# The first stage's preparation reordered over banks and engines, and attention values on two banks

## The chip, the cores and the metric

The kernel runs on one core of one Trainium2 chip. The metric is the device time of one execution in microseconds; the median of the runs is compared. One execution was taken by the hardware profiler; its times are counted from the first instruction of its span.

## The reference

The program computes two transformer-like blocks on x, 512 tokens by 1024, all in float32. The change touches the beginning of the first block:

```python
h = concatenate([lead, meta, x])                 # 16 meta tokens are real
a = rmsnorm(h, g_mix)
proj = einsum('bld,de->ble', a, w_in)            # 1024 x 3584, seven parts of 512 columns
sb_q, sb_k, sb_v, hg_q, hg_f, hg_i, hg_g = split(proj)
# stick-breaking attention, 8 heads of 64:
w = where(valid, exp(log_beta + log_tail), 0)
o = einsum('bhts,bhsd->bhtd', w, v)
```

Behind it come a gated linear recurrence on the other four parts, an output product, a mixture of 32 experts, and a second block (convolution, state-space scan, feed-forward). None of these is changed.

## The kernel before

Engines are programmed by hand: every engine has its own instruction list, in a fixed order, and they meet at semaphores. The eight PSUM banks of 512 float32 per partition are `banks[0]` to `banks[7]`.

**First stage (`stage_a`).** A float32 product is made of three float32r products: each operand is split in a high part (a rounded copy, ScalarE) and a low part (the difference, VectorE). The 512 tokens are four tiles of 128 rows, the meta tokens a fifth (`TILES`, L131). For each tile ScalarE squares and sums the row (L216) and takes the root (L219); VectorE takes the reciprocal (L307) and multiplies row, root and norm weights `gbc` into one of two `xn` buffers (L311); TensorE turns the tile by eight 128x128 transposes (L366) into banks 6 and 7; ScalarE copies each bank as `aT_hi` (L244), and VectorE subtracts to get `aT_lo` (L299). As all tiles use banks 6 and 7, a tile's turn waits until the lower part of the one before is made (L363).

The weights `w_in` come in 14 units of 1 MB (`units`), loaded by SP into three `raw` buffers (L164), split by ScalarE in `make_hi` (L238) and by VectorE in `make_lo` (L293) into two pairs `whi`, `wlo`. SP loads unit u once `make_lo` of unit u-3 is done (L156). On TensorE all five turns come first, then unit zero (L382 on), then the small vectors' four transposes (`vectors`, L354), then the other units. Unit zero and one are the 512 columns of q.

The order on ScalarE before: DMA of the meta rows (L191), DMA of the norm weights (L192), five times square and root, four constants for the attention (L224 to L228), fourteen DMAs that bring small vectors into `vrow` (L232), then the copies of the turned tiles, with the high part of unit zero behind tile 1 and of unit one behind tile 2. Then, unit by unit, the evacuation of the products; behind unit zero's stand two sigmoids of a gate constant (L280), behind each unit's the high part of the unit two further on. VectorE waits for the norm weights first, and its order is norm of tile j, lower part of tile j-1, low part of unit j-3. GpSimd makes masks at the start and then is free.

**Attention (first part of the next stage).** Eight heads, each in three pieces of 384, 384 and 512 columns, so 24 pieces. A piece's scores go into one of `RING` = 6 banks (L481 to L493), ScalarE takes three functions of it (`front`, L554), VectorE makes sums and splits them (`sums`, L658), TensorE adds the tails into the same bank (`tails`, L495), and ScalarE takes the exponential into `ww` (`weights`, L574), upon which the bank is free. TensorE runs three pieces ahead with the scores. The products with v of a head (`values`, L513) all go into bank 7, `O`, and wait until VectorE has copied the earlier head out (`out_evacuate`, L687). Bank 6 holds the meta tokens' scores.

Of the kernel before, what the change touches and what calls it, by code (L numbers as in the profile page):

```python
# [5 lines left out]
ALU = mybir.AluOpType  # L6
ACT = mybir.ActivationFunctionType
AX = mybir.AxisListType
F32 = mybir.dt.float32
# [4 lines left out]
P = 128  # L14
T = 512
NEVER = 2.0 ** 30
NT = T // P
D = 1024
KD = D // P
META = 16  # L20
# [50 lines left out]
def stage_a(nc, dram, g, sem, banks):  # L71
# [5 lines left out]
    with ExitStack() as keep:  # L77
        def sb(name, shape, dt=F32, ctx=None):
# [19 lines left out]
            "it xor xf up ge mask never".split())}  # L98
        s_x = [sem(f"a_x{i}") for i in range(NT)]
        s_raw = [sem(f"a_raw{i}") for i in range(3)]  # L100
        with ExitStack() as tmp:
# [45 lines left out]

            block = tmp.enter_context(nc.Block())

            @block.sync  # L150
            def _(sp):
                for i in range(NT):
                    sp.dma_start(h[:, i, :], x_t[:, i, :]).then_inc(s_x[i], 16)
                for u, (n, what, turned, half) in enumerate(units):
                    if u >= 3:
                        sp.wait_ge(s["wlo"], u - 2)  # L156
                    c = n * 512
                    if turned:
                        src = w_in[:, :, c + half * 256:c + half * 256 + 256]
                        dst = raw[u % 3].rearrange("p (k c) -> p k c", k=KD)  # L160
                    else:
                        src = w_in[:, half * 4:half * 4 + 4, c:c + 512]
# [24 lines left out]

            @block.scalar
            def _(act):
                act.wait_ge(s["hm0"], 1)  # L190
                act.dma_start(hm[0:META, :], dram["meta_tokens"]).then_inc(s["meta"], 16)  # L191
                act.dma_start(gbc, dram["g_mix"][0].partition_broadcast(P)).then_inc(s["gbc"], 16)  # L192
                srcs = {
                    "lb": dram["lb_logits"].rearrange("l (c p) -> (l c) p", p=P),
                    "sb_gain": dram["sb_gain"].rearrange("l (c p) -> (l c) p", p=P),
                    "hg_gain": dram["hg_gain"].rearrange("l (c p) -> (l c) p", p=P),
                    "gate_b": dram["gate_b_2"].rearrange("l (c p) -> (l c) p", p=P),
                    "glu_b": dram["glu_b_2"].rearrange("l (c p) -> (l c) p", p=P),
                    "dw_b": dram["conv_dw_b_2"].rearrange("l (c p) -> (l c) p", p=P),
                    "ln_g": dram["conv_ln_g_2"].rearrange("l (c p) -> (l c) p", p=P),  # L200
                    "ln_b": dram["conv_ln_b_2"].rearrange("l (c p) -> (l c) p", p=P),
                    "pw_b": dram["conv_pw_b_2"].rearrange("l (c p) -> (l c) p", p=P),
                    "ssm_b": dram["ssm_conv_b_2"].rearrange("l (c p) -> (l c) p", p=P),
                    "norm_g": dram["ssm_norm_g_2"].rearrange("l (c p) -> (l c) p", p=P),
                    "dw_w_a": dram["conv_dw_w_2"][0].rearrange("k (c p) -> (k c) p", p=P)[0:128],
                    "dw_w_b": dram["conv_dw_w_2"][0].rearrange("k (c p) -> (k c) p", p=P)[128:CONV_K * 8],
                    "ssm_w": dram["ssm_conv_w_2"][0].rearrange("k (c p) -> (k c) p", p=P),
                }

                act.wait_ge(s["eps"], 1)  # L210
                for j, i in enumerate(TILES):
                    if i == NT:
                        act.wait_ge(s["meta"], 16)
                    else:
                        act.wait_ge(s_x[i], 16)
                    nc.scalar.activation(sq[:, :], hm if i == NT else h[:, i, :], ACT.Square,  # L216
                                         accum_out=ssq[:, i:i + 1]).then_inc(s["ssq"], 1)
                    act.wait_ge(s["ssq"], j + 1)
                    nc.scalar.activation(rt[:, i:i + 1], ssq[:, i:i + 1], ACT.Sqrt, bias=eps[:, 0:1],  # L219
                                         scale=1.0 / D).then_inc(s["rt"], 1)  # L220
                act.wait_ge(s["never"], 2)
# [7 lines left out]
                for t, tile in enumerate(VEC_TILES):  # L229
                    at = 0  # L230
                    for name, n in tile:
                        act.dma_start(vrow[at:at + n, t, :], srcs[name]).then_inc(s["vec"], 16)  # L232
                        at += n
                def make_hi(u):
                    act.wait_ge(s_raw[u % 3], 16 * (u // 3 + 1))
                    if u >= 2:
                        act.wait_ge(s["wused"], u - 1)
                    nc.scalar.copy(whi[u % 2][:, :], raw[u % 3]).then_inc(s["whi"], 1)  # L238


                for j, i in enumerate(TILES):
                    for half in range(2):
                        act.wait_ge(s["tr"], 2 * j + half + 1)
                        nc.scalar.copy(aT_hi[:, 4 * half:4 * half + 4, i * P:i * P + P],  # L244
                                       banks[6 + half][:, :].rearrange("p (k t) -> p k t", k=4)).then_inc(s["hi"], 1)
                    if 1 <= j < 3:
                        make_hi(j - 1)
# [38 lines left out]
            def _(dve):  # L286
# [9 lines left out]
                def lower(j, i):  # L296
                    for half in range(2):
                        dve.wait_ge(s["hi"], 2 * j + half + 1)
                        nc.vector.tensor_tensor(aT_lo[:, 4 * half:4 * half + 4, i * P:i * P + P],  # L299
                                                banks[6 + half][:, :].rearrange("p (k t) -> p k t", k=4),  # L300
# [3 lines left out]
                dve.wait_ge(s["gbc"], 16)  # L304
                for j, i in enumerate(TILES):
# [7 lines left out]
                    if j >= 1:  # L313
                        lower(j - 1, TILES[j - 1])
                    if j >= 3:
                        make_lo(j - 3)
                lower(4, TILES[4])
# [29 lines left out]
            def _(pe):  # L347
# [12 lines left out]
                for j, i in enumerate(TILES):  # L360
                    pe.wait_ge(s["xn"], j + 1)
                    for half in range(2):
                        if j >= 1:  # L363
# [5 lines left out]
                pe.wait_ge(s["lo"], 10)  # L369
# [68 lines left out]
        NP, WIDTH, AHEAD, RING = 3 * SB_HEADS, 1280, 3, 6  # L438
        s = {n: sem("b_" + n) for n in (
            "zm z ab u l k q t w o oev con conr qs qhi own vb kb vr vm abm um lm spm tm wm om mo osq ossq ort ors on f kx q1 dec tab").split()}  # L440
        with ExitStack() as tmp:
# [17 lines left out]
            ZM, O = pall[:, 6, :], pall[:, 7, :]  # L459
# [17 lines left out]
            def _(pe):  # L477
# [53 lines left out]
                for n in range(NP):  # L531
# [3 lines left out]
                    if n == 0:  # L535
# [5 lines left out]
                        mm(O, pick[:, :, :].rearrange("k h s -> k (h s)"), v_nat[0:META, NT, :], start=True,  # L541
# [108 lines left out]
            def _(dve):  # L650
# [30 lines left out]
                def values_meta():  # L681
                    dve.wait_ge(s["vr"], 1)
                    dve.wait_ge(s["own"], 3)
                    V.tensor_tensor(vb[:, :, :], O.rearrange("p (h d) -> p h d", h=SB_HEADS),
                                    own_rows[:, :].unsqueeze(2).to_broadcast([P, SB_HEADS, SB_DIM]), ALU.mult).then_inc(s["vm"], 1)

                def out_evacuate(hd):  # L687
                    dve.wait_ge(s["o"], hd + 1)
                    V.tensor_copy(o_sb[:, :, hd * SB_DIM:hd * SB_DIM + SB_DIM],
                                  O[:, 0:NT * SB_DIM].rearrange("p (i d) -> p i d", i=NT)).then_inc(s["oev"], 1)  # L690
# [2328 lines left out]
```

## Time and profile before

| | |
|---|---|
| Median of three runs | 2304.44 us (2299.78 to 2311.39) |
| The profiled execution | 2295.25 us, its span 2293.2 us |
| TensorE busy | 2061.0 us, 90% of the span |
| VectorE, ScalarE, GpSimd busy | 1363.3, 1069.2, 167.6 us |
| Mean granted TensorE clock | 0.941 |
| First product of unit zero | 35.35 us |
| Attention starts | 224.2 us |

The profile page gives busy times over the whole span; the rows below are from stretches of it. PE is TensorE's matmul queue, PEld its weight loads, DVE VectorE, ACT ScalarE, POOL GpSimd, SP SyncE, and a trailing q is the engine's instruction queue (DMA issues). PEclk is the share of full TensorE clock that was granted.

### The profile page before, as it was taken

How to read it: one execution, taken by the hardware profiler on the slowest of the kernel's cores; microseconds unless marked ns; L12 is line 12 of the kernel's file. 1: busy time of each engine (PE TensorE's matmuls, PEld its weight loads, DVE VectorE, ACT ScalarE, POOL GpSimd, SP SyncE). 2: the span in 40 equal slices, each digit the busy share in tenths (PEclk: the TensorE clock that was granted, in tenths of full speed). 3: DMA queues.
4: the chain of work that ended last, by engine and by line, in shares of the span. 5: the costliest groups of instructions: out<-in, count | busy, mean ns of one | idle time of the engine just before them, and what ended most of it. 6: DMA issues, size and time to landing. Idle time of an engine off the chain costs nothing. (4 is left out here: it accounts for less than half of the span.)

```text
span 2293.2 us, 25099 instructions
## 1 busy us (share of the span) xinstructions
PE 2061.0 (90%) x10173; PEld 1640.2 (72%) x10173; DVE 1363.3 (59%) x1511; ACT 1069.2 (47%) x1253; POOL 167.6 (7%) x129
## 2 busy tenths in 40 slices
PE   5999987879999999947799999988698988999997
PEld 4887666756666666636688888877487866888786
DVE  4111777489989988943398888876533254333213
ACT  4223533468888888833334455545241233222212
POOL 0000100012213222200000000000000000000000
PEclk9999799989999999976999999999899988999999
DMA  4220003379999999951333333322222212333221
GB/s 149 86 74 0 1 1 121 131 271 407 405 402 400 402 403 402 363 200 51 93 86 96 94 93 92 93 74 56 68 79 92 92 56 83 96 105 93 90 94 56
DMA packets 201776, 346.84 MB, mean 151 GB/s; under 512 B 13587, under 2 KB 149259, under 8 KB 184251
## 3 DMA queue, kind: packets, MB, share of 16 engines
q1 hardware_dynamic: 193508, 333.16, 41.4%
q0 software_dynamic: 5120, 8.40, 1.1%
q10 hardware_dynamic: 3031, 3.65, 0.5%
q8 instruction: 82, 1.34, 0.2%
q14 instruction: 35, 0.29, 0.0%
HBM read 340.91 MB, written 12.65 MB: 154 GB/s over the span
## 5 line engine op out<-in xcount | busy, mean ns | idle before, releaser
L1453 DVE TENSOR_TENSOR wlo_e<-raw_e,whi_e 128x2048 fp32r<-128x2048 f32 x190 | 431.8, 2288 | 56.2 <-ACT whi_e L1378 55.6
L1750 DVE TENSOR_TENSOR w_lo<-w_raw,w_hi 128x2048 fp32r<-128x2048 f32 x89 | 203.8, 2290 | 321.1 <-ACT w_hi L1742 321.1
L1378 ACT CAST whi_e<-raw_e 128x2048 fp32r<-128x2048 f32 x188 | 359.3, 1912 | 73.5 <-PE pall L1529 44.9
L1742 ACT CAST w_hi<-w_raw 128x2048 fp32r<-128x2048 f32 x89 | 169.4, 1904 | 428.4 <-PE pall L50 414.2
L48 PE MATMUL pall<-hT_hi,w_lo 128*128 128x512 f32 x864 | 347.8, 403 | 22.9 <-DVE xbc L2294 10.3
L49 PE MATMUL pall<-hT_lo,w_hi 128*128 128x512 f32 x864 | 341.6, 395 | 0.0
L50 PE MATMUL pall<-hT_hi,w_hi 128*128 128x512 f32 x864 | 341.1, 395 | 0.0
L1528 PE MATMUL pall<-whi_e,xs 128*128 128x512 f32 x512 | 210.2, 411 | 3.0 <-DVE xs L1458 3.0
L48 PEld LDWEIGHTS pall<-hT_hi,w_lo 128*128 128x128 f32 x864 | 165.9, 192 | 59.7 <-DVE xbc L2294 10.6
L1529 PE MATMUL pall<-wlo_e,xs 128*64 128x512 f32 x512 | 206.1, 403 | 0.0
L50 PEld LDWEIGHTS pall<-hT_hi,w_hi 128*128 128x128 f32 x864 | 165.5, 192 | 35.5
L49 PEld LDWEIGHTS pall<-hT_lo,w_hi 128*128 128x128 f32 x864 | 166.0, 192 | 34.6 <-issue 0.5
L1528 PEld LDWEIGHTS pall<-whi_e,xs 128*128 128x128 f32 x512 | 99.5, 194 | 54.8 <-issue 4.5
L2279 DVE SCALAR_TENSOR_TENSOR mixed<-yT,cols,mixed 128x512 f32<-128x512 f32 x180 | 126.4, 748 | 0.0
L48 PE MATMUL pall<-w_hi,hT_lo 128*128 128x256 f32 (+1 forms) x320 | 100.0, 313 | 8.8 <-DVE hT_lo L2740 8.4
L48 PE MATMUL pall<-whi_e,hT_lo 128*64 128x512 f32 x256 | 101.4, 396 | 5.7 <-issue 4.1
L50 PE MATMUL pall<-whi_e,hT_hi 128*64 128x512 f32 x256 | 101.1, 395 | 0.0
L49 PE MATMUL pall<-wlo_e,hT_hi 128*64 128x512 f32 x256 | 100.8, 394 | 0.0
L49 PE MATMUL pall<-w_lo,hT_hi 128*128 128x256 f32 (+1 forms) x320 | 98.8, 309 | 0.0
L50 PE MATMUL pall<-w_hi,hT_hi 128*128 128x256 f32 (+1 forms) x320 | 98.6, 308 | 0.0
L2897 DVE TENSOR_TENSOR mixed<-mixed,pall 128x512 f32<-128x512 f32 x22 | 15.1, 688 | 139.9 <-PE pall L50 139.9
L1529 PEld LDWEIGHTS pall<-wlo_e,xs 128*64 128x64 f32 x512 | 70.9, 138 | 21.6
(468 smaller groups left out, 3807.3 us busy)
## 6 DMA issues: line engine op xcount, KB each, us to landing
raw_e<-in_w_expert_up_dram SPq DMA_DIRECT2D x64, 1024.0 KB, 11.1
raw_e<-in_w_expert_down_dram SPq DMA_DIRECT2D x64, 1024.0 KB, 11.5
raw_e<-in_w_expert_gate_dram SPq DMA_DIRECT2D x64, 1024.0 KB, 11.5
w_raw<-in_w_in_dram SPq DMA_DIRECT2D x80, 512.0 KB, 5.9
w_raw<-in_w_gate_up_dram SPq DMA_DIRECT2D x44, 512.0 KB, 5.1
w_raw<-in_w_down_dram SPq DMA_DIRECT2D x22, 512.0 KB, 4.1
mixed<-in_w_in_dram SPq DMA_DIRECT2D x10, 1024.0 KB, 5.1
A<-acs_rows SPq DMA_DIRECT2D x8, 1024.0 KB, 5.0
```

Source lines behind the costliest of these rows:

```text
L48: nc.tensor.matmul(out, w_lo, m_hi, start=start, stop=False)
L49: nc.tensor.matmul(out, w_hi, m_lo, start=False, stop=False)
L50: return nc.tensor.matmul(out, w_hi, m_hi, start=False, stop=stop)
L1378: nc.scalar.copy(whi[j], raw[j]).then_inc(sem_hi, 1)
L1453: nc.vector.tensor_tensor(wlo[j], raw[j], whi[j].bitcast(F32), ALU.subtract).then_inc(sem_lo, 1)
L1528: mm(out, x[:, kk, :], k4(whi[j])[:, k, :], start=kk == 0, stop=False, skip_group_check=True)
L1529: last = mm(out[0:SLOTS, :], x[:, kk, 0:SLOTS], k4(wlo[j])[:, k, :], start=False, stop=kk == KD - 1, skip_group_check=True)
L1742: self.nc.scalar.copy(self.hi[i][:, :], self.raw[i][:, :]).then_inc(self.s_hi, 1)
L1750: (engine or self.nc.vector).tensor_tensor(self.lo[i][:, :], self.raw[i][:, :], self.hi[i][:, :].bitcast(F32), ALU.subtract).then_inc(self ...
L2279: ins = V.scalar_tensor_tensor(mixT[:, c, :], src, col("dw_w_a", k * KD + c), mixT[:, c, :], ALU.mult, ALU.add)
L2897: V.tensor_tensor(hd, sg, banks[(2 * c + 1) % 8], ALU.mult).then_inc(s["hd"], 1)
```

## The change

In the first stage the norm weights' DMA becomes ScalarE's first instruction, followed by a load of the function table that has square and root. The small vectors' fourteen DMAs move from ScalarE's queue to SP's, behind the loads of the first three units. The four tiles of tokens are turned into own pairs of banks (0 and 1, 2 and 3, 4 and 5, 6 and 7), so the turns no longer wait for the lower parts; the meta tile is turned behind unit zero. ScalarE makes the high part of unit zero behind tile 0's copies, the constants come last. The low part of unit zero is made by GpSimd. In the attention the ring has five banks, and the values alternate between bank 5 and bank 7.

```diff
+            def turn_bank(j):
+                return 2 * j if j < NT else 6
+            def made_lo(u):
+                return (s["wlo0"], 1) if u == 0 else (s["wlo"], u)
             @block.sync
...
+                    if u == 3:
+                        for t, tile in enumerate(VEC_TILES):
+                            at = 0
+                            for name, rows_n in tile:
+                                sp.dma_start(vrow[at:at + rows_n, t, :], srcs[name]).then_inc(s["vec"], 16)
+                                at += rows_n
                     if u >= 3:
-                        sp.wait_ge(s["wlo"], u - 2)
+                        sp.wait_ge(*made_lo(u - 3))
...
+                pool.wait_ge(s["whi"], 1)
+                nc.gpsimd.tensor_tensor(wlo[0][:, :], raw[0], whi[0][:, :].bitcast(F32), ALU.subtract).then_inc(s["wlo0"], 1)
             @block.scalar
             def _(act):
+                act.dma_start(gbc, dram["g_mix"][0].partition_broadcast(P)).then_inc(s["gbc"], 16)
+                nc.scalar.preload_act_table_set("sqrt_and_others")
                 act.wait_ge(s["hm0"], 1)
                 act.dma_start(hm[0:META, :], dram["meta_tokens"]).then_inc(s["meta"], 16)
-                act.dma_start(gbc, dram["g_mix"][0].partition_broadcast(P)).then_inc(s["gbc"], 16)
...
+                root(0)
+                root(1)
+                root(2)
+                root(3)
+                upper(0)
+                make_hi(0)
+                upper(1)
+                upper(2)
+                upper(3)
+                root(4)
+                make_hi(1)
+                upper(4)
                 act.wait_ge(s["never"], 2)
...
             @block.vector
...
+                dve.wait_ge(s["gbc"], 16)
+                normed(0)
+                normed(1)
+                normed(2)
+                lower(0)
+                normed(3)
+                lower(1)
+                lower(2)
+                lower(3)
+                normed(4)
+                make_lo(1)
+                lower(4)
             @block.tensor
...
+                def turn(j):
                     pe.wait_ge(s["xn"], j + 1)
                     for half in range(2):
-                        if j >= 1:
-                            pe.wait_ge(s["lo"], 2 * (j - 1) + half + 1)
                         for k in range(4):
-                            last = nc.tensor.transpose(banks[6 + half][:, k * P:k * P + P],
+                            last = nc.tensor.transpose(banks[turn_bank(j) + half][:, k * P:k * P + P],
...
+                for j in range(NT):
+                    turn(j)
+                pe.wait_ge(s["lo"], 2 * NT)
                 o = 0
                 for u, (n, what, turned, half) in enumerate(units):
                     if u == 1:
+                        turn(NT)
                         vectors()
                     if u == 2:
                         pe.wait_ge(s["cols"], 1)
-                    pe.wait_ge(s["wlo"], u + 1)
+                        pe.wait_ge(s["lo"], 2 * NT + 2)
+                    pe.wait_ge(*made_lo(u))
...
-        NP, WIDTH, AHEAD, RING = 3 * SB_HEADS, 1280, 3, 6
+        NP, WIDTH, AHEAD, RING = 3 * SB_HEADS, 1280, 3, 5
...
-            ZM, O = pall[:, 6, :], pall[:, 7, :]
+            ZM, O_OF, OM = pall[:, 6, :], (pall[:, 5, :], pall[:, 7, :]), pall[:, 7, :]
...
                 def values(hd):
                     pe.wait_ge(s["w"], 3 * hd + 3)
-                    if hd == 0:
+                    if hd == 1:
                         pe.wait_ge(s["vm"], 1)
-                    else:
-                        pe.wait_ge(s["oev"], hd)
-                    w = ww[hd % 2]
+                    if hd >= 2:
+                        pe.wait_ge(s["oev"], hd - 1)
+                    w, O = ww[hd % 2], O_OF[hd % 2]
```

`root(j)` is square and root of tile j, `upper(j)` and `lower(j)` its high and low copies, `normed(j)` its reciprocal and product into `xn`, with the same instructions and waits as before; `turn_bank` gives their bank. `srcs`, the table of the vectors' places in memory, is unchanged and now stands ahead of the engines' lists. The meta part's helpers name bank 7 as `OM`, and `out_evacuate` reads `O_OF[hd % 2]`.

## Rows read from the trace of the kernel before

**Rows 1.** Busy time in a stretch: from:to, us, then busy (count) by engine, PEclk, DMA.

```profile
100.00:150.00 50.00, 50.00 (x235) 41.80 (x235) 9.17 (x4) 15.65 (x16) 0.00 (x0) 1.00 0.28 91
```

**Rows 2.** Timeline, start to first squares: start us, us, engine line operation out<-in.

```profile
0.79 1.82 SPq L153 DMA_DIRECT2D h<-in_x_dram  x4
...
2.47 0.46 ACTq L192 DMA_DIRECT2D hg_nat<-in_g_mix_dram  x1
2.65 2.63 SPq L164 DMA_DIRECT2D mixed<-in_w_in_dram  x2
...
4.36 1.28 ACT L216 ACT_TABLE_LOAD   x1 [4.36 <-DMA h<-in_x_dram]
...
8.31 1.04 ACT L216 ACTIVATE sq_a<-h 128x1024 f32<-128x1024 f32 x1
...
11.04 1.04 ACT L216 ACTIVATE sq_a<-h 128x1024 f32<-128x1024 f32 x1
```

**Rows 3.** Timeline, from the norm weights to unit zero's first product.

```profile
10.43 0.16 DVE L307 RECIPROCAL rs_a<-rt_a 128x1 f32<-128x1 f32 x1 [8.45 <-DMA hg_nat<-in_g_mix_dram]
...
10.63 1.28 DVE L311 SCALAR_TENSOR_TENSOR xn_a<-h,rs_a,hg_nat 128x1024 f32<-128x1024 f32 x1
...
12.06 1.94 PE L366 MATMUL pall<-ident,xn_a 128*128 128x128 f32 x8 [12.06 <-DVE xn_a L311]
...
13.76 0.54 ACTq L232 DMA_DIRECT2D vrow<-in_lb_logits_dram  x1
...
19.48 1.07 ACT L244 CAST aT_hi<-pall 128x512 fp32r<-128x512 f32 x2 [4.50 <-issue]
...
23.40 1.90 ACT L238 CAST whi_a<-mixed 128x2048 fp32r<-128x2048 f32 x1
...
25.82 1.29 DVE L299 TENSOR_TENSOR aT_lo<-pall,aT_hi 128x512 fp32r<-128x512 f32 x2 [0.20 <-ACT aT_hi L244]
...
35.35 0.80 PE L393 MATMUL pall<-aT_hi,wlo_a 128*128 128x512 f32 x1 [1.96 <-DVE aT_lo L299]
```

**Rows 4.** ScalarE's DMA queue, 7 to 10 us; landings of norm weights, x, units zero and one.

```profile
q10 hardware_dynamic: 142, 0.52, 46.5%
...
DMA to landing us min/median/max: 7.9/7.9/7.9
...
DMA to landing us min/median/max: 3.5/5.2/8.0
...
DMA to landing us min/median/max: 10.7/11.9/13.2
```

**Rows 5.** Timeline, GpSimd's products in the attention and VectorE beside them.

```profile
255.06 4.55 POOL L641 TENSOR_TENSOR q<-hqT,hfT 128x2048 f32<-128x2048 f32 x1 [27.36 <-ACT hfT L582]
255.12 4.77 DVE L673 CAST qh<-qq 128x512 fp32r<-128x512 f32 x1
...
262.35 0.56 DVE L664 SCALAR_TENSOR_TENSOR qq<-pall,ll 128x384 f32<-128x384 f32 x1
```

**Rows 6.** Timeline, between unit zero and unit one, and unit two's low part.

```profile
47.73 0.60 PE L354 MATMUL pall<-ident,vrow 128*128 128x128 f32 x4
...
48.08 0.48 PE L393 MATMUL pall<-aT_hi,wlo_a 128*128 128x512 f32 x1
...
52.43 2.28 DVE L293 TENSOR_TENSOR wlo_a<-raw_a,whi_a 128x2048 fp32r<-128x2048 f32 x1
```

**Rows 7.** Busy time in two stretches of the attention, three pieces (one head) each.

```profile
265.80:281.60 15.80, 15.32 (x47) 10.86 (x46) 10.63 (x23) 6.18 (x12) 0.00 (x0) 0.53 0.01 1
281.60:290.17 8.57, 8.57 (x46) 6.21 (x46) 5.17 (x12) 6.16 (x12) 0.00 (x0) 1.00 0.00 0
```

**Rows 8.** Timeline of the attention: a wait of the values; weights, then scores.

```profile
267.61 4.50 PE L523 MATMUL pall<-v_nat,ww 128*128 128x64 f32 x20 [0.48 <-DVE mixed L689]
...
295.81 0.47 ACT L579 ACTIVATE ww<-pall 128x384 f32<-128x384 f32 x1
...
297.65 0.33 PE L486 MATMUL pall<-keep_r,ident_r 128*128 128x384 f32 x1
```

More of the change, by code:

```diff
@@ L97, in stage_a @@
             "x meta vec gbc ident ones eps hm0 ssq rt rs xn tr hi lo vtr cols lbd lb whi wlo wused out evac "
-            "it xor xf up ge mask never".split())}
+            "it xor xf up ge mask never wlo0".split())}
         s_x = [sem(f"a_x{i}") for i in range(NT)]
@@ L146, in is_meta_turned @@
                 return what in ("k", "hf")
+            def turn_bank(j):
+                return 2 * j if j < NT else 6
             block = tmp.enter_context(nc.Block())
+            def made_lo(u):
+                return (s["wlo0"], 1) if u == 0 else (s["wlo"], u)
+            srcs = {
+                "lb": dram["lb_logits"].rearrange("l (c p) -> (l c) p", p=P),
+                "sb_gain": dram["sb_gain"].rearrange("l (c p) -> (l c) p", p=P),
+                "hg_gain": dram["hg_gain"].rearrange("l (c p) -> (l c) p", p=P),
+                "gate_b": dram["gate_b_2"].rearrange("l (c p) -> (l c) p", p=P),
+                "glu_b": dram["glu_b_2"].rearrange("l (c p) -> (l c) p", p=P),
+                "dw_b": dram["conv_dw_b_2"].rearrange("l (c p) -> (l c) p", p=P),
+                "ln_g": dram["conv_ln_g_2"].rearrange("l (c p) -> (l c) p", p=P),
+                "ln_b": dram["conv_ln_b_2"].rearrange("l (c p) -> (l c) p", p=P),
+                "pw_b": dram["conv_pw_b_2"].rearrange("l (c p) -> (l c) p", p=P),
+                "ssm_b": dram["ssm_conv_b_2"].rearrange("l (c p) -> (l c) p", p=P),
+                "norm_g": dram["ssm_norm_g_2"].rearrange("l (c p) -> (l c) p", p=P),
+                "dw_w_a": dram["conv_dw_w_2"][0].rearrange("k (c p) -> (k c) p", p=P)[0:128],
+                "dw_w_b": dram["conv_dw_w_2"][0].rearrange("k (c p) -> (k c) p", p=P)[128:CONV_K * 8],
+                "ssm_w": dram["ssm_conv_w_2"][0].rearrange("k (c p) -> (k c) p", p=P),
+            }
             @block.sync
@@ L186, in _, with root @@
                                         pattern=[[1, P]], channel_multiplier=-1).then_inc(s["never"], 1)
+                pool.wait_ge(s["whi"], 1)
+                nc.gpsimd.tensor_tensor(wlo[0][:, :], raw[0], whi[0][:, :].bitcast(F32), ALU.subtract).then_inc(s["wlo0"], 1)
             @block.scalar
             def _(act):
+                act.dma_start(gbc, dram["g_mix"][0].partition_broadcast(P)).then_inc(s["gbc"], 16)
+                nc.scalar.preload_act_table_set("sqrt_and_others")
                 act.wait_ge(s["hm0"], 1)
                 act.dma_start(hm[0:META, :], dram["meta_tokens"]).then_inc(s["meta"], 16)
-                act.dma_start(gbc, dram["g_mix"][0].partition_broadcast(P)).then_inc(s["gbc"], 16)
[L193 to L208, printed above, removed]
                 act.wait_ge(s["eps"], 1)
-                for j, i in enumerate(TILES):
+                def root(j):
+                    i = TILES[j]
                     if i == NT:
@@ L215, in _ @@
                         act.wait_ge(s_x[i], 16)
+                    if j >= 1:
+                        act.wait_ge(s["ssq"], j)
                     nc.scalar.activation(sq[:, :], hm if i == NT else h[:, i, :], ACT.Square,
@@ L220, in _, with make_hi, upper @@
                                          scale=1.0 / D).then_inc(s["rt"], 1)
+                def make_hi(u):
+                    act.wait_ge(s_raw[u % 3], 16 * (u // 3 + 1))
+                    if u >= 2:
+                        act.wait_ge(s["wused"], u - 1)
+                    nc.scalar.copy(whi[u % 2][:, :], raw[u % 3]).then_inc(s["whi"], 1)
+                def upper(j):
+                    i = TILES[j]
+                    for half in range(2):
+                        act.wait_ge(s["tr"], 2 * j + half + 1)
+                        nc.scalar.copy(aT_hi[:, 4 * half:4 * half + 4, i * P:i * P + P],
+                                       banks[turn_bank(j) + half][:, :].rearrange("p (k t) -> p k t", k=4)).then_inc(s["hi"], 1)
+                root(0)
[10 more added lines that the diff above has]
+                upper(4)
                 act.wait_ge(s["never"], 2)
@@ L228, in _ @@
                                      scale=0.0)
[L229 to L247, printed above, removed]
                 def evacuate(o):
@@ L294, in make_lo, with lower @@
                                             ALU.subtract).then_inc(s["wlo"], 1)
-                def lower(j, i):
+                def lower(j):
+                    i = TILES[j]
                     for half in range(2):
@@ L299, in lower, with normed @@
                         nc.vector.tensor_tensor(aT_lo[:, 4 * half:4 * half + 4, i * P:i * P + P],
-                                                banks[6 + half][:, :].rearrange("p (k t) -> p k t", k=4),
+                                                banks[turn_bank(j) + half][:, :].rearrange("p (k t) -> p k t", k=4),
                                                 aT_hi[:, 4 * half:4 * half + 4, i * P:i * P + P].bitcast(F32),
                                                 ALU.subtract).then_inc(s["lo"], 1)
-                dve.wait_ge(s["gbc"], 16)
-                for j, i in enumerate(TILES):
+                def normed(j):
+                    i = TILES[j]
                     dve.wait_ge(s["rt"], j + 1)
@@ L312, in _ @@
                                                    gbc, ALU.mult, ALU.mult).then_inc(s["xn"], 1)
-                    if j >= 1:
[L314 to L317, printed above, removed]
+                dve.wait_ge(s["gbc"], 16)
[10 more added lines that the diff above has]
+                lower(4)
                 dve.wait_ge(s["vtr"], 1)
@@ L358, in _ @@
                 pe.wait_ge(s["ident"], 2)
-                for j, i in enumerate(TILES):
+                def turn(j):
                     pe.wait_ge(s["xn"], j + 1)
                     for half in range(2):
-                        if j >= 1:
-                            pe.wait_ge(s["lo"], 2 * (j - 1) + half + 1)
                         for k in range(4):
-                            last = nc.tensor.transpose(banks[6 + half][:, k * P:k * P + P],
+                            last = nc.tensor.transpose(banks[turn_bank(j) + half][:, k * P:k * P + P],
                                                        xn[j % 2][:, (4 * half + k) * P:(4 * half + k + 1) * P], ident[:, :])
                         last.then_inc(s["tr"], 1)
-                pe.wait_ge(s["lo"], 10)
+                for j in range(NT):
+                    turn(j)
+                pe.wait_ge(s["lo"], 2 * NT)
                 o = 0
@@ L540, in _ @@
                         pe.wait_ge(s["vb"], 1)
-                        mm(O, pick[:, :, :].rearrange("k h s -> k (h s)"), v_nat[0:META, NT, :], start=True,
+                        mm(OM, pick[:, :, :].rearrange("k h s -> k (h s)"), v_nat[0:META, NT, :], start=True,
                            stop=True).then_inc(s["vr"], 1)
@@ L683, in values_meta @@
                     dve.wait_ge(s["own"], 3)
-                    V.tensor_tensor(vb[:, :, :], O.rearrange("p (h d) -> p h d", h=SB_HEADS),
+                    V.tensor_tensor(vb[:, :, :], OM.rearrange("p (h d) -> p h d", h=SB_HEADS),
                                     own_rows[:, :].unsqueeze(2).to_broadcast([P, SB_HEADS, SB_DIM]), ALU.mult).then_inc(s["vm"], 1)
@@ L689, in out_evacuate @@
                     V.tensor_copy(o_sb[:, :, hd * SB_DIM:hd * SB_DIM + SB_DIM],
-                                  O[:, 0:NT * SB_DIM].rearrange("p (i d) -> p i d", i=NT)).then_inc(s["oev"], 1)
+                                  O_OF[hd % 2][:, 0:NT * SB_DIM].rearrange("p (i d) -> p i d", i=NT)).then_inc(s["oev"], 1)
                 def keys(e):
```

## The prediction

> **What bounds the kernel now.** I read the table of stretches first. In the first stage's products (100 to 150 us) TensorE is busy for all 50.00 us, so a product is never waited for; its first product starts only at 35.35 us [rows 1, 3]. Every microsecond by which that start moves forward is therefore a microsecond of the time, as long as nothing later eats it. Next the timeline of the stretch before it. The order there is: x lands in four tiles, ScalarE squares them, VectorE waits for the norm weights until 10.43, TensorE turns the first tile at 12.06, and then ScalarE, which has to copy the turned tile, is issuing DMAs: the first of the vectors' DMAs goes out at 13.76 and the first copy comes at 19.48 [rows 2, 3]. After that the five tiles go through one pair of banks, one after another, with the splitting of units zero and one in between. Last the attention: a head takes 8.57 us at granted clock 1.00, with TensorE busy throughout, and 15.80 us at 0.53 [rows 7]; TensorE bounds it too.
>
> **The first stage, step by step (times from the span's start).**
> 1. Norm weights. Their DMA goes out at 2.47 and lands 7.9 later, at 10.4; between 7 and 10 us its queue moved 0.52 MB and took 46.5% of the DMA engines [rows 2, 4], so once its turn comes it gets about half. After the change it is ScalarE's first instruction, near 1.0, and only the first tile of x is ahead. Shared with one or two tiles it lands at 5.5 to 6.5; with the latency of before, at 8.9. I take 6.2. The DMA was the wait of VectorE; what is late next is x.
> 2. Table. One load of 1.28 us stands behind the first tile's landing at 4.36 [rows 2]; a second one follows the first square. The change makes it one, done while x is in flight. The squares after the second load need none, so one set serves both functions. Worth nothing by itself: the fourth tile of x is issued near 2.2 and lands 8.0 later, at 10.2 [rows 2, 4], and with the weights ahead of it the sum of bytes up to there is the same. Squares come every 1.37 us ((11.04 - 8.31) / 2, [rows 2]), so the four roots are done at 10.2 + 1.4 = 11.6.
> 3. Splitting unit zero. ScalarE makes the upper halves of tile 0 (1.07 for two copies [rows 3]), to 12.7, and then the high part of unit zero. That waits for the load, which was issued at 2.65 and landed 10.7 later, at 13.35 [rows 2, 4]; x, weights and meta rows are ahead of it as before, so this stands. 13.35 + 1.90 for the copy [rows 3] = 15.3. GpSimd takes over the low part: it waits for this copy and has nothing queued behind; the nearest row is its product of the same 128x2048 shape, 4.55 us [rows 5]. 15.4 + 4.55 = 20.0, and TensorE starts unit zero at 20.1. Bounds: 19.4 if the load is in before ScalarE is free, 21.3 if GpSimd first waits for a VectorE instruction of 1.28 us.
> 4. The tiles beside it. VectorE norms tile 0 to 2 by 12.1, lowers tile 0 (1.29 for the pair, [rows 3]) to 13.4, and norms tile 3 (reciprocal 0.16, product 1.28) from 13.4 to 14.9. TensorE turns tile 3 in 1.94 [rows 3] to 17.0. ScalarE is free of unit zero at 15.3 and copies tiles 1 to 3 in 3 x 1.07, to 18.5; the last lowering ends at 19.2. So TensorE waits for GpSimd, by 0.8 us; that is the margin of these tiles.
> 5. The meta tile's turn moves behind unit zero, onto TensorE's path. The vectors' four turns take it from 47.73 to 48.08 [rows 6], 0.35; eight at that pace cost 0.7. Upper bound 1.94, the cold duration. Its norming (root five on ScalarE, 18.5 to 19.9) and unit one's halves (ScalarE to 21.8, VectorE to 24.1) lie under unit zero, which runs to 32.
> 6. What queues behind. ScalarE now waits for the meta tile's turn, and behind it stand the six 0.3 to 0.6 us copies it did early before, the evacuations of unit zero, the gate constants and then the high part of unit two. Before, unit two's low part started at 52.43 and took 2.28 [rows 6], done 6.6 after unit one's start at 48.08; unit zero, with its slow beginning, took 12.4 (35.35 to 47.73, [rows 3, 6]), unit one takes about 11. After the change about 2.3 us more stand in ScalarE's queue there, so it is done some 8.9 after: 2 us of slack are left. Cost nothing; if the cover fails, rival B.
> 7. The fourteen vector DMAs on SP's queue: issue time some 0.35 each, 10.2 to 15.2, then SP waits for GpSimd's part at 20.0. Unit three's load, behind them, took 5.0 us at that place before, so it lands at 25; its split is wanted after 44. The vectors are wanted at 32. Nothing.
> 8. The waits dropped between tiles (own banks) are contained in these times.
> Start of unit zero 35.35 - 20.1 = 15.25 earlier, less 0.7: 14.5. The half-speed products at the beginning of unit zero stay.
>
> **Attention.** Five banks in the ring instead of six: the scores of a piece wait for the weights of one piece later. The tightest place in a head: weights done at 295.81 + 0.47 = 296.28, the scores that will need them start at 297.65 [rows 8], 1.37 later; in the other two pieces of a head it is more. So this wait holds nobody: cost zero, and that is the upper end unless the order shifts. Two value banks: TensorE waited for the earlier head's evacuation once, 0.48 us, before the values at 267.61 [rows 8]; this wait goes. TensorE is the bound there, so 0.5 gained. The lower end is nothing.
>
> **Sum.** 14.5 + 0.5 = 15.0. The profiled execution took 2295.25 (span 2293.2); it becomes 2280.2. The median of the three runs shown is 2304.44, 9.2 above that execution, and 2289.4 is what I forecast for it.
>
> **A lock that speaks against it.** When GpSimd began its 4.55 us product at 255.06, VectorE's cast at 255.12 took 4.77, while the VectorE instruction with one operand in PSUM ran in 0.56 beside GpSimd's next products [rows 5]. By this the lowerings (one operand in PSUM) run beside GpSimd, but tile 3's norming has x and the weights, both in SBUF. The Trainium skill, "SBUF — State Buffer", section "SBUF: two separate sides", says the pair of ports that VectorE and GpSimd share is an exclusive lock, taken also by a VectorE instruction with two SBUF inputs, and whoever starts first holds it for the whole instruction; the trace's cast agrees, and for a norming no run here shows it.
>
> **Rivals.**
> A. GpSimd gets in first. If tile 3's norming starts after 15.4 instead of 13.6, it is held to 20.0: norm to 21.3, turn to 23.2, copy and lowering to 24.7. Start 4.6 later, gain 10.4: 2294.0. For it: the weights landing only at 8.9 (latency as before) puts that norming at 15.1 to 15.4, the very edge. Against: half of the queue's rate from 2 us on, and 1.8 us of room. 0.12.
> B. Unit two comes late: step 6 short of slack by 2 to 3 us. Gain 12.5: 2292. For it: ScalarE's queue is in order and the slack is my estimate. 0.08.
> C. Slower than before. The place is the attention: the stretch at half clock [rows 7] comes right behind the stall of [rows 5], and a shorter one stands at the stage's start. Each further head at it costs 15.80 - 8.57 = 7.2 us [rows 7]. It decides from the point where more than two heads (15.0 / 7.2) are added; if five that now run at full clock fall, +36 - 15 = +21: 2325. For it: the clock already falls twice in this stage. Against: full clock comes back at 281.6 under the same load, and the ring adds no idle time. 0.05 (slower), and 0.05 for one or two heads, which ends near no change.
> D. The other way: with the stages shifted, one head less at half clock, gain 22: 2282. 0.07.
> E. The forecast, 2289.4: 0.63.
>
> **Range and chances.** E alone, with a start between 19.4 and 21.3, the meta turn up to 1.94 and the runs' own spread of some 5 us: 2283 to 2296. Taking in A, B and D: 2279 to 2300. Of this kernel's runs (2299.78 to 2311.39) about 0.5%, 11.5 us, can be told from no change, so 2292.9 is the edge: E is above it only in one case of seven; A is just beyond, B just within. Faster 0.70, same 0.24, slower 0.06.
>
> **What would show it.** First product of unit zero at 20.1 (right from 19.4 to 21.3), released by GpSimd; weights landed by 6.5; one table load before the first square; tile 3's norming 1.28 us long, not 5; unit one's first product 14.5 earlier than 48.08; products of unit two without a gap; no wait of scores for weights; from there on the two traces run parallel, 15 us apart. Wrong if the start is later than 24, if TensorE stands still before unit two, or if the attention runs longer or shorter at a granted clock of 0.5 than before.

## The result and the profile after

The changed kernel takes 2277.41 us at the median of its first four runs (2271.61 to 2279.0) against 2302.11 for the kernel before; the ratio is 0.9893, 95% interval 0.9865 to 0.9921. Two repetitions gave 0.9929 [0.9907, 0.9951] and 0.9905 [0.9882, 0.9928]. Over all 16 runs of it the mean is 2278.8, over 60 runs of the kernel before 2298.5 (standard deviations 4.2 and 4.7): 19.6 us faster. The forecast was 2289.4, faster by 15.0, with 2279 as its lower end: the direction and the mechanism of the first stage came out, the time is 1.6 us under the range.

The profiled execution took 2279.0 us, its span 2276.8, 16.4 less than before. Its timeline, for [rows 2] and [rows 3]:

```profile
0.78 0.40 ACTq L221 DMA_DIRECT2D hg_nat<-in_g_mix_dram  x1
0.79 2.11 SPq L176 DMA_DIRECT2D h<-in_x_dram  x4
...
1.21 1.28 ACT L222 ACT_TABLE_LOAD   x1 [1.21 <-PEq L3047]
...
6.59 1.06 ACT L235 ACTIVATE sq_a<-h 128x1024 f32<-128x1024 f32 x1 [4.10 <-DMA h<-in_x_dram]
...
8.18 0.16 DVE L335 RECIPROCAL rs_a<-rt_a 128x1 f32<-128x1 f32 x1 [6.19 <-ACT rt_a L238]
...
9.81 5.31 PE L400 MATMUL pall<-ident,xn_a 128*128 128x128 f32 x24 [9.81 <-DVE xn_a L339]
...
12.56 1.06 ACT L251 CAST aT_hi<-pall 128x512 fp32r<-128x512 f32 x2
...
14.03 1.90 ACT L245 CAST whi_a<-mixed 128x2048 fp32r<-128x2048 f32 x1 [0.41 <-DMA mixed<-in_w_in_dram]
...
14.55 1.28 DVE L339 SCALAR_TENSOR_TENSOR xn_a<-h,rs_a,hg_nat 128x1024 f32<-128x1024 f32 x1
...
16.01 4.58 POOL L217 TENSOR_TENSOR wlo_a<-mixed,whi_a 128x2048 fp32r<-128x2048 f32 x1 [12.99 <-ACT whi_a L245]
...
16.44 3.68 DVE L327 TENSOR_TENSOR aT_lo<-pall,aT_hi 128x512 fp32r<-128x512 f32 x6 [0.60 <-ACT aT_hi L251]
...
20.74 0.76 PE L432 MATMUL pall<-aT_hi,wlo_a 128*128 128x512 f32 x1 [3.75 <-POOL wlo_a L217]
...
33.82 1.03 PE L400 MATMUL pall<-ident,xn_a 128*128 128x128 f32 x8
...
34.69 0.60 PE L390 MATMUL pall<-ident,vrow 128*128 128x128 f32 x4
...
35.04 0.48 PE L432 MATMUL pall<-aT_hi,wlo_a 128*128 128x512 f32 x1
```

The reader is to see that each link named in the prediction is there. VectorE's first wait ends with ScalarE's root, no longer with the weights' DMA. Tile 0's copies come at 12.56 instead of 19.48. ScalarE then waits for unit zero's load (14.03), GpSimd follows at 16.01, and unit zero starts at 20.74, released by GpSimd, with the lowerings done at 20.12. Behind it stand the meta tile's turn (33.82 to 34.69, 0.87) and the vectors. Two repetitions of the kernel start unit zero at 20.54 and 20.50.

Stretches of the same kernel: the first products of unit zero, the attention's first 13 us, and its second half-clock stretch, which answers to [rows 7].

```profile
20.70:25.10 4.40, 4.36 (x10) 3.46 (x11) 3.33 (x2) 1.31 (x1) 0.00 (x0) 0.50 0.73 238
...
211.21:224.00 12.79, 12.79 (x26) 6.46 (x27) 9.77 (x25) 8.66 (x17) 2.94 (x13) 0.60 0.01 1
...
245.50:267.60 22.10, 19.72 (x57) 13.35 (x57) 17.30 (x31) 9.81 (x19) 6.60 (x8) 0.61 0.00 1
```

How far ahead of the kernel before it is at each landmark: unit zero 14.6 us, unit one (48.08 - 35.04) 13.0, attention (224.23 - 211.21) 13.0, the recurrence behind it (325.09 - 311.66) 13.4, end of the span 16.4. The last 3.0 lie where nothing was changed: from the start of the recurrence to the end it takes 1968.1 us in `before` and 1965.1 here, but 1965.8 in `before_again` and 1968.5 in the two repetitions of the changed kernel. So they are scatter.

### The profile page after: what moved, and what is told of

Same layout as the page of the kernel before. It is cut to its first block and busy times, and to the rows that moved or that the text cites. A ratio compares the mean times of both kernels' runs of the same rounds, so it can differ in the third digit from the quotient of the medians.

```text
span 2276.8 us, 25098 instructions
## 1 busy us (share of the span) xinstructions
PE 2054.9 (90%) x10173; PEld 1636.9 (72%) x10173; DVE 1361.3 (60%) x1510; ACT 1066.6 (47%) x1252; POOL 173.3 (8%) x130
## 3 DMA queue, kind: packets, MB, share of 16 engines
HBM read 340.91 MB, written 12.65 MB: 155 GB/s over the span
## 5 line engine op out<-in xcount | busy, mean ns | idle before, releaser
L971 POOL DMA_INDIRECT xg<-m_rows,row_x x32 | 81.8, 2557 | 67.4 <-PE pall L1558 36.2
```

Of the source, the lines that this page charges most:

```text
L971: pool.indirect_dma_start(xg[0:SLOTS, :], None, m_rows, bass.IndirectOffsetOnAxis(g["row_x"][0:SLOTS, b:b + 1], 0), bounds_check=T - 1, oo ...
```

## The experiments

**Both kernels again, and each part alone.** The first two are the kernels unchanged; `first_only` is the first stage of the change with the attention of before, `att_only` the reverse (the diff shows the lines that set the banks; those that follow from them are left out):

```diff
 # first_only
+NP, WIDTH, AHEAD, RING = 3 * SB_HEADS, 1280, 3, 6
+ZM, O = pall[:, 6, :], pall[:, 7, :]
 # att_only: the kernel before, with
+NP, WIDTH, AHEAD, RING = 3 * SB_HEADS, 1280, 3, 5
+ZM, O_OF, OM = pall[:, 6, :], (pall[:, 5, :], pall[:, 7, :]), pall[:, 7, :]
```

> The kernel before, unchanged, as its own yardstick. Both theories: ratio to the kernel before 1.000. It also gives a second profile of it. Theory one (the true gain of the change is about 15, and the 24.7 between the medians comes from runs of the kernel before that differ by 20 us among themselves): the runs of this kernel scatter again over more than 10 us, and its second profile differs from the first in the lengths of half-clock stretches, not in the first 35 us, where unit zero starts again at 35.35 within 0.3. Theory two (the true gain is about 25): the profile of before, 2295.25, was a lucky run, and this one's profile is nearer to 2302.

> The changed kernel, unchanged, timed again. Theory one, gain of 15: ratio 0.9935, that is 2287 against 2302. Theory two, gain of 25: ratio 0.989. Unit zero starts at 20.7 within 0.3 in this profile too.

> The change's first stage with the attention of before (six score banks, one value bank). Theory one: 0.5 us slower than the full change, not to be told from it, ratio 0.994; unit zero at 20.7, attention start 13.0 earlier than 224.2, one 0.5 us wait of the values in front of an evacuation. Rival: the attention part is worth the missing 9 us, then this one is at 0.993 and the full change at 0.989.

> The kernel before with the attention part of the change alone (five score banks, two value banks). Theory one: ratio 1.000 (0.5 us faster), the values' wait for the evacuation gone, no wait of scores for weights. Rival: ratio 0.996, 9 us faster, visible as fewer or shorter half-clock stretches in the attention.

> The changed kernel a third time, to settle the size of its gain: 0.9893 [0.9865, 0.9921] at first, 0.9929 [0.9907, 0.9951] the second time. Gain of 16 (stage starts 13 to 14 us earlier, attention 1 to 3 by its clock): 0.993. Gain of 25: 0.989. In the profile unit zero starts at 20.6 within 0.3.

Measured: `before_again` 1.001 [0.9994, 1.0026] over 12 runs from 2293.69 to 2308.22; `after_again` 0.9929; `first_only` 0.9939 [0.9917, 0.9961]; `att_only` 0.9991 [0.9978, 1.0004]; `after_third` 0.9905. The kernel before scatters by 15 us in itself, so the first theory holds in that; but neither size is confirmed: the three ratios of the change mean 0.9909, about 21 us, between 15 and 25.

The first stage is most of the change: by the means, `first_only` is 14.1 us faster than the 24 runs of the kernel before beside it. The standard error, the expected error of such a difference from the scatter of its runs, is 2.1 us. The attention part is small and hard to see. The ratio of `att_only` includes no change, its mean is 3.1 us lower (standard error 1.3), and the changed kernel's mean is 4.6 lower than that of `first_only` (2.2). A gain of 9 us is ruled out.

Much of the scatter is the clock, and each run has its mean granted clock on record. The span times (1 - clock) is the time that a run loses to the half clock, about half the length of its stretches at 0.5. With this time taken off, `att_only` is 2.7 us faster than the 57 runs of the kernel before that have a clock (standard error 0.7). So the attention part is worth more than the 0.5 of the forecast. A part of it is the wait of the values for the earlier head's evacuation. It was 0.48 in `before` [rows 8], and here it is in `before_again` and in `first_only`, both with one value bank:

```profile
268.56 4.40 PE L523 MATMUL pall<-v_nat,ww 128*128 128x64 f32 x20 [1.99 <-DVE mixed L689]
...
255.08 4.50 PE L562 MATMUL pall<-v_nat,ww 128*128 128x64 f32 x20 [2.00 <-DVE mixed L728]
```

With two banks, in `att_only` and the changed kernel, the wait is gone (in `vec_moved`, with one bank, there is none either). In single profiles the attention's length (100.86 us in `before`, 101.20 in `before_again`, 100.45 in `att_only`; 100.45, 96.70 and 101.44 in the changed kernel) is too scattered to show the gain.

**The vectors' DMAs.** These two kernels and the next four were run once each; their times (2274.68 to 2296.65 us) differ by little more than the two kernels scatter, so they are read by the start of unit zero in their traces, and say nothing of the whole time. `vec_back` starts from the changed kernel, `vec_moved` from the kernel before; the loops are shortened here:

```diff
 # vec_back: taken from SP, and on ScalarE
                 root(3)
+                for t, tile in enumerate(VEC_TILES): ... act.dma_start(vrow[...], srcs[name])
                 upper(0)
 # vec_moved: taken from ScalarE, and on SP
+                    if u == 3:
+                        for t, tile in enumerate(VEC_TILES): ... sp.dma_start(vrow[...], srcs[name])
```

> The changed kernel with the vectors' fourteen DMAs on ScalarE again, ahead of tile 0's copies. My theory (before, ScalarE's DMA issues held the copies): root four is done at 12.6, the issues take 5.7 us (13.76 to 19.44 before), tile 0's copies start at 18.3, unit zero's high part at 19.3, GpSimd ends at 25.8, unit zero's first product at 26, 5.3 later than 20.7. Rival (the issues are hidden, the own banks or the earlier weights made the gain): 21 to 22.

> The kernel before with only the vectors' DMAs moved to SP. My theory: tile 0's copies start when the four constants are done, 15.0 instead of 19.48, and all that follows is 4.5 earlier: unit zero at 30.9 instead of 35.4. Rival (hidden): 35.

The timelines of `vec_back`, then of `vec_moved`:

```profile
12.37 0.53 ACTq L255 DMA_DIRECT2D vrow<-in_lb_logits_dram  x1
...
18.02 1.07 ACT L245 CAST aT_hi<-pall 128x512 fp32r<-128x512 f32 x2 [5.36 <-issue]
...
25.94 0.77 PE L431 MATMUL pall<-aT_hi,wlo_a 128*128 128x512 f32 x1 [2.59 <-POOL wlo_a L211]
```

```profile
15.03 1.04 ACT L246 CAST aT_hi<-pall 128x512 fp32r<-128x512 f32 x2
...
30.87 0.79 PE L395 MATMUL pall<-aT_hi,wlo_a 128*128 128x512 f32 x1 [1.97 <-DVE aT_lo L301]
```

Unit zero at 25.94 (26 expected) and 30.87 (30.9): ScalarE's DMA issues are worth 4.5 us from the one side and 5.2 from the other. "Idle until issue" in front of a copy is what such a wait looks like.

**The lock.** All three start from the changed kernel; `norm3_beside` was made to test rival A's mechanism, the others for a part of the change each:

```diff
 # norm3_beside (VectorE)
                 lower(0)
-                normed(3)
                 lower(1)
+                normed(3)
 # weights_late (ScalarE)
                 act.dma_start(hm[0:META, :], dram["meta_tokens"]).then_inc(s["meta"], 16)
+                act.dma_start(gbc, dram["g_mix"][0].partition_broadcast(P)).then_inc(s["gbc"], 16)
 # one_pair
-                return 2 * j if j < NT else 6
+                return 6
+                        if j >= 1:
+                            pe.wait_ge(s["lo"], 2 * (j - 1) + half + 1)
```

> The changed kernel with one swap in VectorE's order: tile 3's norming after tile 1's lowering, so that it meets GpSimd's 4.6 us product (16.0 to 20.6). Lock theory (rival A of the prediction): lowerings with a PSUM operand run beside GpSimd in their 0.65; the norming, both operands in SBUF, is held from 17.9 to 20.6 and the record is about 4 us long instead of 1.28; unit zero at 24.7. No lock for this instruction: 1.28 long, unit zero at 21.8.

> The changed kernel with the norm weights' DMA behind the meta rows' again, as before (issue near 2.4 us). My theory: they land near 10.3 instead of before 8.2; tile 0 is normed at 10.5 instead of 8.4, tile 3's norming starts at 16.7, inside GpSimd's product, is held to 20.6, and unit zero starts at 24.7. If the weights' order doesn't matter: 20.7. If it matters but nothing is held: 21.

> The changed kernel with all tiles turned into banks 6 and 7 and the waits on the lower parts back. My theory: each turn waits for the lowering before it, the last lowering ends near 22.9, unit zero at 23.0, 2.3 later. If own banks are worth nothing: 20.7; if they are the main part of the gain: 30 or later.

Timelines of `norm3_beside`, of `weights_late`, and of `one_pair`:

```profile
15.79 4.61 POOL L217 TENSOR_TENSOR wlo_a<-mixed,whi_a 128x2048 fp32r<-128x2048 f32 x1 [12.78 <-ACT whi_a L245]
16.23 1.29 DVE L327 TENSOR_TENSOR aT_lo<-pall,aT_hi 128x512 fp32r<-128x512 f32 x2 [2.02 <-ACT aT_hi L251]
...
17.62 3.85 DVE L339 SCALAR_TENSOR_TENSOR xn_a<-h,rs_a,hg_nat 128x1024 f32<-128x1024 f32 x1
...
24.90 0.79 PE L432 MATMUL pall<-aT_hi,wlo_a 128*128 128x512 f32 x1 [1.40 <-DVE aT_lo L327]
```

```profile
10.36 0.16 DVE L335 RECIPROCAL rs_a<-rt_a 128x1 f32<-128x1 f32 x1 [8.38 <-DMA hg_nat<-in_g_mix_dram]
...
16.44 4.59 POOL L217 TENSOR_TENSOR wlo_a<-mixed,whi_a 128x2048 fp32r<-128x2048 f32 x1 [13.42 <-ACT whi_a L245]
...
16.63 5.48 DVE L339 SCALAR_TENSOR_TENSOR xn_a<-h,rs_a,hg_nat 128x1024 f32<-128x1024 f32 x1
...
25.76 0.80 PE L432 MATMUL pall<-aT_hi,wlo_a 128*128 128x512 f32 x1 [1.62 <-DVE aT_lo L327]
```

```profile
15.91 4.63 POOL L217 TENSOR_TENSOR wlo_a<-mixed,whi_a 128x2048 fp32r<-128x2048 f32 x1 [12.89 <-ACT whi_a L245]
15.97 5.65 DVE L339 SCALAR_TENSOR_TENSOR xn_a<-h,rs_a,hg_nat 128x1024 f32<-128x1024 f32 x1 [1.53 <-PE pall L402]
...
28.29 0.79 PE L434 MATMUL pall<-aT_hi,wlo_a 128*128 128x512 f32 x1 [1.40 <-DVE aT_lo L327]
```

The norming lasts 1.28 us alone and 3.85, 5.48 and 5.65 when GpSimd started first: each time it ends 1.1 us behind GpSimd. The lowerings, one operand in PSUM, keep their pace (1.29 for the pair in `norm3_beside`, as before). The Trainium skill ("SBUF — State Buffer", "SBUF: two separate sides") has this as a lock held for the whole instruction; the three traces agree for a VectorE product of two SBUF operands. So rival A's mechanism is real and 4.2 us dear (24.90 against 20.74), and both the early weights and the own banks are needed to stay clear of it. My 24.7 for `weights_late` was 1.1 early: I let the norming end with GpSimd, at 20.6, and it ended at 22.11. My 23.0 for `one_pair` was wrong by 5.3: I had tile 3's norming at 15.8, before GpSimd. It came 0.06 behind it.

**GpSimd or VectorE for unit zero's low part.**

```diff
                 normed(3)
+                dve.wait_ge(s["whi"], 1)
+                nc.vector.tensor_tensor(wlo[0][:, :], raw[0], whi[0][:, :].bitcast(F32), ALU.subtract)
                 lower(1)
```

> The changed kernel with unit zero's low part on VectorE (behind tile 3's norming) instead of GpSimd. My theory: 2.28 us there from 16.0 to 18.3, then six lowerings of 0.62 to 22.0, unit zero at 22.2, so 1.5 later than 20.7: GpSimd is worth 1.5 us only. Rival (GpSimd's 4.6 us product is the bound and VectorE would beat it): 20.3 or earlier.

```profile
15.84 2.29 DVE L347 TENSOR_TENSOR wlo_a<-mixed,whi_a 128x2048 fp32r<-128x2048 f32 x1
18.05 3.67 DVE L325 TENSOR_TENSOR aT_lo<-pall,aT_hi 128x512 fp32r<-128x512 f32 x6
```

Unit zero at 21.77, 1.0 later than with GpSimd, not 1.5: VectorE needs 2.29 instead of 4.58 but then has the six lowerings (3.67) behind it.

**A faster version.** `spread` cuts GpSimd's products in the attention ([rows 5]), of which the first is shown; `spread_warm` also keeps TensorE busy before unit zero:

```diff
+                for e in range(HG_HEADS):
+                    pool.wait_ge(s["q"], 9 + 2 * e)
+                    gp.tensor_tensor(q1[:, e, :], hqT[:, e, :], hfT[:, e, META:TM], ALU.mult)
...
 # spread_warm, behind turn(3)
+                pe.wait_ge(s["lo"], 2)
+                for n in range(28):
+                    nc.tensor.transpose(banks[0][:, 0:P], ident[:, :], ident[:, :])
```

> The changed kernel, and in the attention GpSimd's products (4.55 + 2.13 + 3.8 us in one go, in whose lock VectorE stood 4.77 and 2.32 us) cut into pieces of at most 1.2 us and spread over pieces 8 to 23 by waiting for VectorE's progress. Theory (the stall makes the half-clock stretch behind it): no idle TensorE of over 1 us there, granted clock 1.00 from the ninth piece on, a head every 8.6 us; 10 us faster than the changed kernel, ratio to before 0.989. Rival (the clock falls there without the stall, or the cut products stall VectorE as long in sum): within 2 us of the changed kernel, 0.993.

> The spread kernel, and TensorE turns the identity 28 times into a free bank between tile 3's turn and unit zero (work that nothing reads). In the changed kernel it stands idle there from 17.0 to 20.74 and runs the first ten products of unit zero at granted clock 0.50, until 25.1. Theory (the idle time costs the clock): unit zero's products take 0.227 us each from the first on, unit one's first product comes near 32.6 instead of 34.5 to 35.5, 2.2 us gained: ratio to before 0.9865. Rival (the clock falls after the turns whatever follows): unit one's start stays at 34.5 or later.

`spread`: 2269.99 us, ratio 0.9875 [0.9852, 0.9897]; `spread_warm`: 2267.48 us, 0.9861 [0.9834, 0.9889]. The attention of `spread` in three stretches, and its first cut product:

```profile
210.40:223.00 12.60, 12.60 (x39) 6.21 (x39) 10.71 (x27) 11.20 (x22) 2.95 (x13) 1.00 0.00 1
223.00:245.00 22.00, 22.00 (x114) 15.89 (x114) 17.55 (x34) 19.35 (x38) 2.54 (x2) 1.00 0.00 1
245.00:267.00 22.00, 22.00 (x116) 15.55 (x115) 18.23 (x37) 15.10 (x30) 4.88 (x4) 1.00 0.00 0
...
237.83 1.27 POOL L682 TENSOR_TENSOR q<-hqT,hfT 128x512 f32<-128x512 f32 x1 [23.96 <-DVE ql L720]
```

In these stretches TensorE is busy throughout at full clock; from the attention's start to the recurrence it takes 85.4 us instead of 100.45. The whole kernel doesn't gain these 15 us. By the means `spread` is 8.5 us faster than the changed kernel (standard error 3.0). One reason stands in its profile: a new stretch at half clock in the recurrence, where work that took 43.8 us now takes 47.9:

```profile
334.00:344.40 10.40, 10.40 (x48) 9.85 (x49) 5.62 (x15) 1.76 (x3) 0.00 (x0) 0.51 0.01 2
```

`spread_warm` has this stretch too. Its time can't be told from that of `spread` (means of 2269.5 and 2270.4), but beside `after_third`, timed with it, it is 10.2 us faster (standard error 2.8). So the two together beat the changed kernel; `spread` by itself does so less surely, as its interval overlaps those of the changed kernel.

Of `spread_warm`, the stretch before unit zero and unit zero:

```profile
16.00:20.70 4.70, 4.15 (x36) 3.91 (x36) 4.15 (x9) 4.67 (x10) 4.62 (x1) 1.00 0.97 280
20.70:32.90 12.20, 12.14 (x59) 10.20 (x60) 3.31 (x2) 1.80 (x3) 0.00 (x0) 1.00 0.53 173
```

Unit one starts at 32.99 instead of 35.04, where the stretch of the changed kernel had 0.50 until 25.10. Against `spread`, from which it differs in nothing else (34.23), the gain is 1.2 us. In all 14 other profiles the first 6 to 14 products of unit zero run at half pace; here none does. So it was the idle time before unit zero that cost the clock.

## Why the prediction was right and wrong

- **The start of unit zero (20.1).** Right: 20.74, by the link and in the order named. The load of unit zero landed at 14.0 instead of 13.35; that is the 0.6. (Root four was done at 12.65 instead of 11.6, which this load hid.)
- **The weights' landing.** Right that it stops being a wait, and at 6.4 for 6.2. Wrong that the first tile of x would keep its time: with the weights at 0.78 beside it, it lands at 6.55 instead of 4.36. The slack up to the load of unit zero took this up.
- **The lock.** The one real danger was seen. Its margin held: tile 3's norming began 1.46 before GpSimd.
- **Meta turn (0.7) and unit zero's own length.** The turn costs 0.87. The step "the half-speed products at the beginning of unit zero stay" took as fixed what changes from run to run. The granted clock reads 1.00 in this stretch of the kernel before, so the products' own lengths have to tell; in `before` they fall at 38.08, after 2.7 us:

```profile
37.65 0.63 PE L399 MATMUL pall<-aT_hi,whi_a 128*128 128x512 f32 x1
...
38.40 0.39 PE L398 MATMUL pall<-aT_lo,whi_a 128*128 128x512 f32 x1
```

  In `before_again` it takes 4.4 us, in the three profiles of the changed kernel 4.4, 3.6 and 6.1. Unit zero to unit one takes 12.73 and 13.48 before, 14.30, 13.97 and 15.11 after. On average 13.5 and not 14.5 reach unit one. The trace of the whole stage after that is the same: 176.15 us to the attention before, 176.17 after.
- **Unit two, the vectors on SP, the ring of five.** Nothing waits for them, as said. The vectors' DMAs went out from 11.0 to 18.6 and not to 15.2; the slack took it.
- **Attention (0.5).** No wait of scores for weights: right. The first two profiles differ by 0.4 in this stage, but that this meets the 0.5 is luck, given their scatter. The term was too small: it took the one value wait of the one profile, 0.48, where two others with one bank show 2.0 and one shows none, and the runs give 2.7 for the part. Rivals C and D were about the stage's clock, and that does move: the half-clock stretch in its first 13 us stands in the profiles of `before`, `before_again`, `att_only`, `first_only`, the changed kernel and `after_third`, not in that of `after_again`, whose attention is 96.70 long instead of 100.45. In `norm3_beside` there is none at all, although TensorE stood as idle behind the lock of [rows 5]:

```profile
245.00:250.00 5.00, 2.60 (x11) 1.60 (x10) 4.76 (x6) 2.44 (x6) 4.75 (x5) 1.00 0.00 0
250.00:270.00 20.00, 20.00 (x114) 15.11 (x113) 18.86 (x41) 14.66 (x29) 1.01 (x3) 1.00 0.01 1
```

 Its attention takes 87.91 us. With the idle time, a half-clock stretch comes near or behind it in 11 of 13 profiles, without it (`spread` and `spread_warm`) in neither of two. So cutting the product is a good bet, but that the idle time is needed for the fall is not shown by two profiles, and it doesn't always bring it.
- **The sum: the step that failed.** By the pooled means the forecast is 10.6 above (2289.4 - 2278.8), for two mis-sized terms. The larger is the base, 5.9: I subtracted from the median of three runs, 2304.44, where 60 runs mean 2298.5 and the profiled execution, 2295.25, stood below it. The text named the distance of 9.2 and did not ask which of the two was off. The other 4.7 is the gain, 19.6 instead of 15.0. The pieces that the runs show are 13.5 up to unit one instead of 14.5, 2.7 for the attention part instead of 0.5, and some 3.4 of half clock, for which the sum had nothing. The last is worked out so: the changed kernel loses as much to the half clock as the kernel before, 133.5 us on average (standard errors 1.4 and 0.6), but in its profile 3.4 of that lie at 18.3 to 25.2, where the record of the kernel before reads 1.00. Behind that it loses 3.4 less, with a standard error of 1.5. Why it should stays open. The profiled executions don't show the whole gain: the two of the kernel before have spans of 2293.2 and 2292.1, the three of the changed one 2276.8, 2275.9 and 2281.8, 14.5 apart on average.
- **The range.** Its lower end took the rival with one head less at half clock from the same high base; with the base at 2298.5 it would have held the time. The pooled mean, 2278.8, lies only 0.2 under it; the first four runs happened to be 1.4 lower.

## What to carry to other kernels

Before a stage that TensorE bounds without a gap, list what each engine does until its first product; DMA issues in front of a copy count like work (here 14 took 5.7 us, 0.4 each, not the 0.35 that I reckoned with). Before giving GpSimd a long product, look which VectorE instructions with both operands in SBUF can meet it, since one that starts behind it waits it out; cut it into pieces and tie them to VectorE's progress. Time such a version as a whole, too: of 15 us in a stage, some 8 came through here (standard error 3). And where the profiled execution lies well below the median of three runs, put the base between the two: here 60 runs did. A wait read from one profile can be four times as long in the next.

## What the runs showed of the hardware

An idle TensorE of 2.4 us behind GpSimd's lock stands in 13 profiles. In eleven of them the attention has a stretch of 13.6 to 34.1 us at granted clock 0.5 close by (17.0 in `before` and the changed kernel, 34.1 in `vec_moved`), in two, `norm3_beside` and `vec_back`, there is none near it. The first products of unit zero ran at half pace for 2.7 to 6.1 us in 14 profiles, and not at all when TensorE was kept turning the identity. The Trainium skill ("TensorE: Matmul & The Clock Gate", "Part 1: The HAM clock gate (the "warmup" mystery)") says the number of cold matmuls differs from run to run of one kernel; the traces agree, with 6 and 10 in two profiles of the kernel before and 10, 8 and 14 in three of the changed one. And a broadcast of 512 KB put in front of x delayed x's first tile by 2.2 us, though both were issued within 0.01 us of each other; with the broadcast back at 2.47, in `weights_late`, the first square starts at 4.42 again.
